# Woven layer norms dealt out by halves of products, with the row scaling on another engine

## What is computed

```python
def layer_norm(x, g, b):
    mu = jnp.mean(xf, axis=-1, keepdims=True)
    var = jnp.mean(jnp.square(xf - mu), axis=-1, keepdims=True)
    return ((xf - mu) * lax.rsqrt(var + LN_EPS) * g + b).astype(x.dtype)
...
mix, st = even_mixer(...) if layer % 2 == 0 else odd_mixer(...)
x = layer_norm(DEEPNORM_ALPHA * x + mix, ln1_g[layer], ln1_b[layer])
x = layer_norm(DEEPNORM_ALPHA * x + jnp.square(jax.nn.relu(x @ w1)) @ w2, ln2_g[layer], ln2_b[layer])
```

## Time and profile before

| | us |
|---|---|
| median of 3 runs | 2563.15 |
| the three runs | 2559.9, 2563.15, 2565.43 |
| the profiled execution | 2558.36 |
| its span | 2556.3 |
| TensorE busy | 2449.8 |
| VectorE busy | 915.5 |
| ScalarE busy | 626.4 |
| GpSimd busy | 503.2 |

### The profile page before, as it was taken

How to read it: one execution, slowest core, us unless ns; L and a number is a source line. 1 busy time by engine, 2 the same in 40 slices (tenths; PEclk the granted TensorE clock), 3 DMA queues, 4 the chain that set the end, 5 groups by cost and what they waited for, 6 DMA issues and landing times.

```text
span 2556.3 us, 39457 instructions
## 1 busy us (share of the span) xinstructions
PE 2449.8 (96%) x16054; PEld 2336.8 (91%) x16054; DVE 915.5 (36%) x2028; ACT 626.4 (25%) x1352; POOL 503.2 (20%) x254
## 2 busy tenths in 40 slices
PE   8999998999999999999999788898999999999996
PEld 8888998999999999998999455798999999999995
DVE  3555534322322322326224655434322322222226
ACT  1323305121121121123100566415122022122022
POOL 2111224221221211213212000123311311211210
PEclk9999999999999999999999899999999999999998
DMA  5100411232232232231211756442232222222221
GB/s 180 66 26 26 112 38 62 75 124 66 74 122 66 82 115 71 82 109 62 75 34 67 276 209 247 145 50 69 85 102 77 93 93 82 87 93 83 92 72 70
DMA packets 77269, 240.12 MB, mean 94 GB/s; under 512 B 25184, under 2 KB 42208, under 8 KB 69344
## 3 DMA queue, kind: packets, MB, share of 16 engines
q1 hardware_dynamic: 60480, 167.65, 19.4%
q10 hardware_dynamic: 16688, 71.05, 9.5%
HBM read 224.78 MB, written 81.71 MB: 120 GB/s over the span
## 4 chain that ended last, share of the span: by engine, by line
PE 87%; DVE 6%; ACT 4%; issue 2%; POOL 1%; DMA 1%; SPq 0%; DVEq 0%; ACTq 0%; POOLq 0%
PE PS L1228 77%; PE PS L1257 1%; PE PS L1497 1%; DVE ZN L850 1%; PE PS L1511 1%; PE PS L1536 1%; PE PS L1523 1%; PE PS L1562 1%; PE PS L1273 1%; POOL WS L480 1%; ACT X L563 1%; PE PS L1309 1%; ACT SMB L706 1%; DVE XS L813 1%; PE PS L1334 1%
## 5 line engine op out<-in xcount | busy, mean ns | idle before, releaser
L1228 PE MATMUL PS<-XS,WS 128*128 128x384 f32 (+1 forms) x8208 | 1382.9, 328 | 25.5 <-DVE XS L813 11.3
L1228 PEld LDWEIGHTS PS<-XS,WS 128*128 128x128 f32 x8208 | 1355.2, 188 | 40.1 <-issue 26.4
L480 POOL TENSOR_TENSOR WS<-WR,WS 128x1024 fp32r<-128x1024 f32 x178 | 434.5, 2441 | 1873.3 <-DVE WS L828 1059.9
L1228 PE MATMUL PS<-HID,WS 128*128 128x384 f32 (+1 forms) x4608 | 765.4, 326 | 4.3 <-DVE X L1026 2.6
L1228 PEld LDWEIGHTS PS<-HID,WS 128*128 128x128 f32 x4608 | 758.4, 188 | 6.6 <-DVE X L1026 3.8
L645 ACT ACTIVATE RT<-PS 128x384 f32<-128x384 f32 (+1 forms) x192 | 91.1, 474 | 1116.3 <-PE PS L1228 1116.3
L1007 DVE TENSOR_TENSOR HID<-ST,HID 128x384 fp32r<-128x384 f32 (+1 forms) x192 | 107.5, 560 | 632.1 <-ACT HID L651 632.1
L1026 DVE TENSOR_TENSOR X<-X,PS 128x384 f32<-128x384 f32 (+1 forms) x336 | 177.6, 531 | 401.0 <-PE PS L1228 400.9
L649 ACT ACTIVATE ST<-RT 128x384 f32<-128x384 f32 (+1 forms) x192 | 97.5, 508 | 7.8
L651 ACT ACTIVATE HID<-ST 128x384 fp32r<-128x384 f32 (+1 forms) x192 | 97.7, 509 | 6.1
L493 POOL TENSOR_TENSOR XS<-X,XS 128x384 fp32r<-128x384 f32 (+1 forms) x72 | 68.9, 965 | 93.4 <-ACT XS L567 89.8
(11 more groups left out here) (166 smaller groups left out, 1212.6 us busy)
## 6 DMA issues: line engine op xcount, KB each, us to landing
WR<-in_w SPq DMA_DIRECT2D x178, 512.0 KB, 3.3
out_d_ks<-in_cache_d_k ACTq DMA_DIRECT2D x96, 340.0 KB
out_d_vs<-in_cache_d_v ACTq DMA_DIRECT2D x96, 340.0 KB
KC<-in_kt SPq DMA_DIRECT2D x16, 1024.0 KB, 10.8
VCD<-in_cache_d_v SPq DMA_DIRECT2D x16, 1024.0 KB, 7.2
X<-in_x SPq DMA_DIRECT2D x6, 768.0 KB, 7.4
TH<-in_th SPq DMA_DIRECT2D x4, 1024.0 KB, 11.4
KC<-in_kt SPq DMA_DIRECT2D x8, 512.0 KB, 9.8
```

The costliest lines, as they stand in the source:

```text
L480: pool.tensor_tensor(WS[:, slot, 1, :], WR[:, raw, :], WS[:, slot, 0, :].bitcast(F32), ALU.subtract).then_inc(w_split, 1)
L1228: last = pe.matmul(out[:, 0:gw], WS[:, slot, a, (off + k) * P:(off + k + 1) * P], src[:, b, k, c0:c0 + gw], start=(n == 0), stop=(n == 3 * ...
```

## The change

`ln_weave(l, v)` now has one index v, which counts half units (or the units of a down projection). Three tables say what stands at v: `FRONT_AT` a front, `SCALE_AT` (two later) the scaling of that tile's rows, `BACK_AT` the backs of two chunks. Even v are called inside a unit: `product` gets a function `middle`, called after half of its chunks. In down projections, where v counts whole units, all pieces stand between units. Fronts lie at v = 8, 10, 12, 16, 18, 20, 24, 26, 28; backs at 15 to 18, 23 to 26, 31 to 34.

The scaling of rows moves to ScalarE, as an activation with RS as scale and NM = -mean*RS as bias. VectorE no longer adds epsilon apart (ScalarE has it as the root's bias), its refinement is in three steps, and NM is a fourth. MV, SD, RS, NW and NM are doubled. For groups 1 and 2 of norms 0 and 2 VectorE makes the high part in XS. Norm 3 ends with the same table in place of an order of its own.

```diff
+FRONT_AT = {8 * (g + 1) + 2 * tt: (g, tt) for g in range(3) for tt in range(3)}
+SCALE_AT = {v + 2: gt for v, gt in FRONT_AT.items()}
+BACK_AT = {8 * (g + 1) + 7 + p: (g, (2 * p, 2 * p + 1)) for g in range(3) for p in range(4)}
...
+        def high_by_vector(l, g):
+
+            return l % 2 == 0 and g > 0
...
+            def ln_weave(l, v):
+
+                if v in BACK_AT:
+                    g, chunks = BACK_AT[v]
                     c0, gw = GROUP[g]
-                    for k in BACK_CHUNKS[quarter]:
-                        n = 24 * l + 8 * g + k
-                        if (l, g) == (3, 2) and k % 2:
-                            continue
-                        act.wait_ge(bt_mm, n + 1)
+                    chunks = [k for k in chunks if (l, g) != (3, 2) or k % 2 == 0]
+                    for k in chunks:
+                        act.wait_ge(bt_mm, 24 * l + 8 * g + k + 1)
                         act.activation(X[:, k, c0:c0 + gw], bank(back_bank(l, g, k), gw), ACT.Identity,
                                        scale=col(C_LNG + KC * l + k), bias=col(C_LNB + KC * l + k)).then_inc(b_evac, 1)
-                        if l < 3:
-                            act.wait_ge(b_evac, n + 1)
+                    for k in chunks:
+                        if l < 3 and not high_by_vector(l, g):
+                            act.wait_ge(b_evac, 24 * l + 8 * g + k + 1)
                             act.activation(XS[:, 0, k, c0:c0 + gw], X[:, k, c0:c0 + gw], ACT.Copy).then_inc(b_hi, 1)
-                if "F" in parts and 0 <= phase - 1 <= 2 and quarter > 0:
-                    n = 9 * l + 3 * (phase - 1) + quarter - 1
-                    rows = tile_rows(3 * (phase - 1) + quarter - 1)
-                    act.wait_ge(ve_ready, n + 1)
-                    act.activation(SD[0:rows, :], VE[0:rows, :], ACT.Sqrt).then_inc(std_ready, 1)
+                if v in SCALE_AT:
+                    g, tt = SCALE_AT[v]
+                    n = 9 * l + 3 * g + tt
+                    r = tile_rows(3 * g + tt)
+                    act.wait_ge(rs_ready, n + 1)
+                    if n >= 3:
+                        act.wait_ge(bt_mm, 24 * l + 8 * g - (8 if (l, g) == (3, 2) else 0))
+                    act.activation(rows_out(l, g)[0:r, tt, :], rows_in(l, 3 * g + tt)[0:r, :], ACT.Identity,
+                                   scale=RS[0:r, n % 2:n % 2 + 1], bias=NM[0:r, n % 2:n % 2 + 1]).then_inc(zn_ready, 1)
+                if v in FRONT_AT:
+                    g, tt = FRONT_AT[v]
+                    n = 9 * l + 3 * g + tt
+                    r = tile_rows(3 * g + tt)
+                    act.wait_ge(mv_ready, n + 1)
+                    act.activation(SD[0:r, n % 2:n % 2 + 1], MV[0:r, n % 2, 1:2], ACT.Sqrt,
+                                   bias=EPSC[0:r, :]).then_inc(std_ready, 1)
...
+                        if weave is not None and g < 2:
+                            ln_weave(weave, 24 + 2 * u)
                         act.wait_ge(h_mm, n + 1)
...
-            def ln_weave(l, phase, quarter, parts="BF"):
-                if "F" in parts and 0 <= phase - 1 <= 2 and quarter > 0:
-                    g, tt = phase - 1, quarter - 1
+            def ln_weave(l, v):
+                if v in BACK_AT and high_by_vector(l, BACK_AT[v][0]):
+                    g, chunks = BACK_AT[v]
+                    c0, gw = GROUP[g]
+                    for k in chunks:
+                        dve.wait_ge(b_evac, 24 * l + 8 * g + k + 1)
+                        dve.tensor_copy(XS[:, 0, k, c0:c0 + gw], X[:, k, c0:c0 + gw]).then_inc(b_hi, 1)
+                if v in FRONT_AT:
+                    g, tt = FRONT_AT[v]
                     n = 9 * l + 3 * g + tt
-                    r = tile_rows(3 * g + tt)
+                    r, e = tile_rows(3 * g + tt), slice(n % 2, n % 2 + 1)
                     FT = rows_in(l, 3 * g + tt)
+                    if n >= 2:
+                        dve.wait_ge(zn_ready, n - 1)
                     dve.wait_ge(ft_mm, n + 1)
                     dve.bn_stats(BNS[0:r, 0:6], FT[0:r, 0:512])
                     link(dve.bn_stats(BNS[0:r, 6:12], FT[0:r, 512:1024]))
-                    link(dve.bn_aggr(MV[0:r, :], BNS[0:r, :]))
-                    dve.tensor_scalar(VE[0:r, :], MV[0:r, 1:2], EPS, None, ALU.add).then_inc(ve_ready, 1)
+                    dve.bn_aggr(MV[0:r, n % 2, :], BNS[0:r, :]).then_inc(mv_ready, 1)
                     dve.wait_ge(std_ready, n + 1)
-                    link(dve.reciprocal(RS[0:r, :], SD[0:r, :]))
-
-                    link(dve.scalar_tensor_tensor(out=NW[0:r, :], in0=RS[0:r, :], scalar=VE[0:r, :], in1=RS[0:r, :],
+                    link(dve.reciprocal(RS[0:r, e], SD[0:r, e]))
+
+                    link(dve.scalar_tensor_tensor(out=NW[0:r, e], in0=MV[0:r, n % 2, 1:2], scalar=EPS, in1=RS[0:r, e],
+                                                  op0=ALU.add, op1=ALU.mult))
+                    link(dve.scalar_tensor_tensor(out=NW[0:r, e], in0=NW[0:r, e], scalar=-0.5, in1=RS[0:r, e],
                                                   op0=ALU.mult, op1=ALU.mult))
-                    link(dve.tensor_scalar(NW[0:r, :], NW[0:r, :], -0.5, 1.5, ALU.mult, ALU.add))
-                    link(dve.tensor_tensor(RS[0:r, :], RS[0:r, :], NW[0:r, :], ALU.mult))
-                    if n >= 3:
-                        dve.wait_ge(bt_mm, 24 * l + 8 * g - (8 if (l, g) == (3, 2) else 0))
-                    dve.tensor_scalar(rows_out(l, g)[0:r, tt, :], FT[0:r, :], MV[0:r, 0:1], RS[0:r, 0:1],
-                                      ALU.subtract, ALU.mult).then_inc(zn_ready, 1)
+                    link(dve.scalar_tensor_tensor(out=RS[0:r, e], in0=NW[0:r, e], scalar=1.5, in1=RS[0:r, e],
+                                                  op0=ALU.add, op1=ALU.mult))
+                    dve.scalar_tensor_tensor(out=NM[0:r, e], in0=MV[0:r, n % 2, 0:1], scalar=-1.0, in1=RS[0:r, e],
+                                             op0=ALU.mult, op1=ALU.mult).then_inc(rs_ready, 1)
...
+                        if s == 1:
+                            ln_weave(2 * l, 8 * g + 2 * j)
...
-            def product(out, slot, off, nk, src, g, done, second=None):
+            def product(out, slot, off, nk, src, g, done, second=None, middle=None):
 
                 c0, gw = GROUP[g]
                 n = 0
                 for k in range(nk):
                     if second is not None and k == nk // 2:
                         pe.wait_ge(second, 1)
+                    if middle is not None and k == nk // 2:
+                        middle()
...
+                            v = 8 * g + 2 * j
+                            unit(u0 + 12 * s + 4 * g + j, t0 + 4 * s + j, g,
+                                 (lambda: ln_weave(2 * l, v, done)) if s else None)
                             if s == 1:
-                                ln_weave(2 * l, g, j, done)
+                                ln_weave(2 * l, v + 1, done)
...
-            for j, part in ((1, "F"), (2, "F"), (0, "B"), (1, "B"), (3, "F"), (2, "B")):
-                ln_weave(3, 3, j, done, part)
-            for j in range(3):
-                ln_weave(3, 4, j, done, "B")
+            for v in range(24, 40):
+                ln_weave(3, v, done)
```

More of the change, by code:

```diff
@@ L1208, in _ @@
             mlp(1)
-            for j in range(1, 4):
-                ln_weave(3, 3, j)
+            for v in range(24, 40):
+                ln_weave(3, v)
             c0, gw = GROUP[2]
@@ L1231, in product, with unit @@
                 last.then_inc(done, 1)
-            def unit(u, t, g):
+            def unit(u, t, g, middle=None):
                 if g == 0:
@@ L1238, in unit, with ln_weave @@
                     pe.wait_ge(p_evac, u - 1)
-                product(bank(6 + u % 2), t % NSLOT, 0, KC, XS, g, p_mm, None if u else x_split)
-            def ln_weave(l, phase, quarter, group_done, parts="BF"):
-                if "B" in parts and 0 <= phase - 2 <= 2 and quarter < 3:
-                    g = phase - 2
-                    for k in BACK_CHUNKS[quarter]:
+                product(bank(6 + u % 2), t % NSLOT, 0, KC, XS, g, p_mm, None if u else x_split, middle)
+            def ln_weave(l, v, group_done):
+                if v in BACK_AT:
+                    g, chunks = BACK_AT[v]
+                    for k in chunks:
                         n = 24 * l + 8 * g + k
@@ L1418, in hidden_super @@
                             pe.wait_ge(h_evac, n - 1)
-                        product(bank(4 + u % 2), (t0 + j) % NSLOT, 0, KC, XS, g, h_mm)
-                        if weave is not None and g < 2:
-                            ln_weave(weave, 3 + g, j, done)
+                        woven = weave is not None and g < 2
+                        v = 24 + 2 * u
+                        product(bank(4 + u % 2), (t0 + j) % NSLOT, 0, KC, XS, g, h_mm, None,
+                                (lambda: ln_weave(weave, v, done)) if woven else None)
+                        if woven:
```

(1 more changed line is left out.)

72 lines of the change are left out of this document (35 added, 37 removed).

## The result

| | before | after |
|---|---|---|
| median, us | 2563.64 | 2542.92 |
| range (runs) | 2557.91 to 2565.43 (6) | 2540.6 to 2544.83 (6) |
| the profiled execution | 2558.36 | 2544.43 |
| its span | 2556.3 | 2542.4 |
| VectorE busy | 915.5 | 895.6 |

The change makes the kernel faster: the ratio after to before is 0.9925, with a 95% interval of 0.9914 to 0.9937. That is 20.7 us at the medians. Forecast were 17.3 us and 2545.9 us.

The account below looks back on a forecast made before the run. TensorE, 87% of the chain that ended last, was taken as the bound. Savings of 5.8+2.6+1.3+7.6 = 17.3 us off the median 2563.15 gave 2545.9 us; own range 2540 to 2551, leaving out 2 in 10: 2535 to 2557.

Parts of the forecast that it names:

- The forecast's cause: Turns back in twos, with two banks: turned chunks' waits for ScalarE fall from 13.2 us to under 2.
- The hole: TensorE's wait for GpSimd's low parts before norm 0's first hidden product: 6.4 us, product starting at 26.0.
- the free chain: VectorE's small steps not held beside GpSimd: first hidden product at 24.6 instead of 26.0, hole 5.0 us.
- none on ZN over 0.5: Sign: no wait of turned chunks for the scaled rows ZN exceeds 0.5 us.
- norm 0: Idle and refilling 11.5 us become 7.3, and a second slow product's 1.6 us goes: 5.8 us saved.
- norm 1: Waits of 6.4+1.8 us become 6.8 with refilling, VectorE held in fronts 4 and 5: 1.3 us saved.
- norm 2: The same 4.2 us saving as norm 0, less 1.6 charged behind a longer hole: 2.6 us saved.
- norm 3: Waits of 2.7+0.8 us go, last product to first ZE turn 15.4 for 20.3: 7.6 us saved.
- Rival 1: Around GpSimd's low parts: holding costs nothing and the clock stays up; about 25 us saved, 2538; chance 0.13.
- Rival 2: Casts before splits also held, each of three holes grows by 2.5 us; 5 us saved, 2556; chance 0.18.
- Rival 3: 27 insertions inside products in norms 0 to 2 cost TensorE 18 us; 2563, no change; chance 0.09.
- Rival 4: ScalarE's queue in the hidden stage: root before relu makes 24 us of RT waits; 2580; chance 0.08.

Follow-up runs that it names:

- e3: Changed kernel with turned chunks in portions of three, three and two instead of twos: 2550.99 us, ratio 0.9957 to the kernel before.
- e1: Changed kernel with the pass over 1024 (scaling of rows) back on VectorE, in the same slots: 2548.06 us, ratio 0.9949 to the kernel before.
- e7: Changed kernel with TensorE's pieces of even v behind the unit, so no product is broken in two: 2547.14 us, ratio 0.9949 to the kernel before.
- e4: Changed kernel with its four small steps as `tensor_scalar`, second tensor as scalar operand: 2541.54 us, ratio 0.9924 to the kernel before.
- e12: The changed kernel unaltered, measured and traced again: 2541.84 us, ratio 0.9926 to the kernel before.
- e8: Changed kernel with one-input small steps, GpSimd's eight low parts behind the first split, and norm 3's fronts 6 and 7 earlier: 2534.34 us, ratio 0.9896.
- e2: Changed kernel with the copies into XS back on ScalarE: 2542.19 us, ratio 0.9920 to the kernel before.
- e11: Changed kernel with one-input steps, GpSimd's low parts together, norm 3's end reordered, and copies into XS by ScalarE: 2517.93 us, ratio 0.9834.

## Why the prediction was right

*The forecast's cause held.* Turned chunks wait 2.8 us for banks against "under 2" forecast; 1.9 of it is one place behind norm 3's last product. e3 brings 6.7 us of these waits back and costs 8 us. So the pairs pay, as the sum had it; that they pay more than the other parts is not shown, since 8 against the 6 of e1 (the pass on ScalarE) and e7 (half units) lies inside the scatter.

*The hole.* The place of the first hidden product came within half a microsecond (25.5 to 25.7 against 26.0) and the free chain within 0.1 (e4: 24.5 against 24.6). The step that missed is "none on ZN over 0.5": the held chain of front 5 also makes tile 5's scaling late, so TensorE loses 2.11 us there and then 3.12 at the hole, about 5.2 together where 6.4 stood. Same delay, other place. The holes themselves, 3.1 and 3.8 us, are under the 4 to 7 that the prediction gave as its sign. In norm 0 two misses nearly cancel, which is luck: TensorE stands 1.2 us less than forecast, and the slow matmuls cost 2.6 us where 1.6 was charged.

*Terms.*

| | forecast, us | measured in the traces |
|---|---|---|
| norm 0 | -5.8 | -5.5 |
| norm 1 | -1.3 | -2.8 |
| norm 2 | -2.6 | -3.2 |
| norm 3 | -7.6 | -8.3 |
| sum | -17.3 | -19.8 (medians -20.7) |

In this profile norm 1 was mis-sized most: the last product waited 2.59 for its bank (3.2 said), that for front 4's addition next to nothing (0.8), the hole was 1.17 (2.3). I had all four steps of front 4 held; the trace shows one (0.93), and three of front 5's (0.88, 0.92, 0.92). But the small hole owes much to the slow product ahead of it: in e12, the same kernel, the hole is 2.75, the way from the mark to the next common event (the turn of KTD in the odd mixer) is 179.4 us instead of 178.1, and norm 1 saves about 1.4, as forecast. Norm 0 has such a term, too: the 1.6 us of its second slow product lay behind a wait of 1.26 us for ZN, but in norm 2 of the same trace the product behind the like wait (1.24) took 4.46 us, as any other. How far the clock falls is not set by the wait alone, so these parts agree by luck within 1 or 2 us. In norm 3 it is the way to ZE, 14.75 instead of 15.4. The slow product that I charged behind a longer hole is there in norms 0 and 2: 4.21 and 3.72 us for twelve matmuls against 2.35. The scaling pass was put at 1.2 us, and 30 of them average 1207 ns:

```profile
L586 ACT ACTIVATE ZN<-PS,NM,RS 128x1024 f32<-128x1024 f32 x30 | 36.2, 1207 | 31.7 <-DVE NM L875 31.5
```

*Rival 1 (no holding, 2538):* the holding is real (0.94 us steps), but in e4 taking it from the small steps brought nothing measurable. The rival's mechanism is wrong and its worth was overrated too: with the small steps free, the casts and TensorE's earlier arrival fill the gap. My own free-chain bound (1.6 us more at each of norms 0 and 2) made the same error.

*Rival 2 (GpSimd's chain grows, 2556):* casts are held, as it said (2.66 and 2.21), but behind the point that sets the hole. Where the hole is gone (e8) they become what decides.

*Rival 3 (broken products, 2563):* 2 us in place of 18. The 0.33 us that stood before a weight load of 64 rows does not add up either: six turns with a tile of 64 rows take 1.09 us to the start of the next product, before (445.90 to 446.99) as after (432.16 to 433.25).

*Rival 4 (ScalarE's queue, 2580):* no wait for RT anywhere. Its mechanism, a root ahead of ScalarE's other work, did appear in e8, but at the evacuation and not at the relu, 6 us in each of two norms.

## What to carry to other kernels

Two waits that one chain feeds hide each other. Here three edits that measured 0, 3 and 4 us brought 7 together, because a new wait of 6.0 us in each of two norms came where the hole had been; and moving the copies, worth nothing in the changed kernel (e2), brought 16 us more on top of them (e11). An edit that measures as nothing is worth a second try once the wait behind which it hid is gone, and its stretch in the trace (mark to mark) tells sooner than the total. Move work onto VectorE only after asking whether GpSimd runs beside it: here a two-input step took 0.94 us beside a low part and 2.18 beside a split instead of 0.16, and a float32 weight cast 2.66 instead of 0.69. A `tensor_scalar` with scalar operands from SBUF was not held (214 ns). And read a gain of a few us from several executions or from stretches, not from one profile: the same kernel's stretch of norm 1 differed by 1.4 us between two.
